# A Fourier mixer on 256 token rows instead of 512, and a modulation that comes one place later

## What is computed

```python
e = rms_norm(p @ w_ple_proj, ple_norm_gain)
x = x + sigmoid(x @ w_ple_gate) * e
...
mod = silu(c) @ w_ada[i] + b_ada[i]
sh1, sc1, g1, sh2, sc2, g2 = split(mod, 6)
h = rmsnorm(x, norm_mix_g) * (1 + sc1) + sh1
hg = h.reshape(B, S, 4, 256)
f = fft.fftn(hg, axes=(1, 3), norm="ortho").real
x = x + g1 * (f.reshape(B, S, 1024) @ w_fourier_out)
h = rmsnorm(x, norm_ffn_g) * (1 + sc2) + sh2
x = x + g2 * swiglu(h, w_ffn_in, w_ffn_out)
```

## Time and profile before

| what | us |
|---|---|
| median of 3 runs | 1541.34 (1540.82 to 1541.92) |
| the profiled execution | 1540.15 |
| its span in the trace | 1538.2 |
| PE busy in the span | 1526.9 |
| DVE, ACT, POOL busy | 786.8, 632.4, 876.3 |
| from the first gate residual on DVE to the last square sum | 299.4 to 320.3 |
| first matmul of the Fourier output | 342.28 |

### The profile page before, as it was taken

One profiled execution on the slowest core, in us unless ns is written; L12 is line 12 of the kernel. 1 busy time (PEld: TensorE's weight loads), 2 busy tenths in 40 slices (PEclk: granted clock), 3 DMA queues, 4 the chain that ended last, 5 costly groups with the idle time before them and its releaser, 6 DMA issues.

```text
span 1538.2 us, 21352 instructions
## 1 busy us (share of the span) xinstructions
PE 1526.9 (99%) x7242; PEld 1276.9 (83%) x7242; DVE 786.8 (51%) x1176; ACT 632.4 (41%) x1038; POOL 876.3 (57%) x1040
## 2 busy tenths in 40 slices
PE   9999999999999999999999999999999999999997
PEld 7888888898888888888888888888889888888886
DVE  7887787876654544541554435356257454011113
ACT  7444444674533333323444334253345333122223
POOL 6555557556577766775454535526435766555551
PEclk9999999999999999999999999999999999999999
DMA  7544455335355555542232322213312553222321
GB/s 247 178 145 165 167 192 191 110 110 178 122 180 205 196 190 181 199 150 96 101 103 69 108 69 94 95 52 96 95 55 83 205 205 123 96 96 95 95 82 55
DMA packets 58267, 202.99 MB, mean 132 GB/s; under 512 B 6496, under 2 KB 8544, under 8 KB 58208
## 3 DMA queue, kind: packets, MB, share of 16 engines
q1 hardware_dynamic: 56912, 198.87, 37.8%
q10 hardware_dynamic: 1296, 3.30, 0.6%
HBM read 200.05 MB, written 2.10 MB: 131 GB/s over the span
## 4 chain that ended last, share of the span: by engine, by line
PE 78%; POOL 11%; issue 9%; ACT 0%; DMA 0%; DVE 0%; SPq 0%; POOLq 0%; DVEq 0%; ACTq 0%
PE banks L1785 21%; PE banks L1789 21%; PE banks L1788 21%; POOL w_lo L423 11%; PE banks L2270 2%; PE banks L2269 2%; PE banks L2266 2%; PE banks L1801 2%; PE banks L1804 2%; PE banks L1805 2%; PE banks L2306 1%; PE banks L2304 1%; PE banks L2305 1%; PE banks L2293 0%; PE banks L2292 0%
## 5 line engine op out<-in xcount | busy, mean ns | idle before, releaser
L423 POOL TENSOR_TENSOR w_lo<-w_raw,w_hi 128x256 fp32r<-128x256 f32 x1028 | 868.9, 877 | 627.8 <-ACT w_hi L455 627.7
L455 ACT ACTIVATE w_hi<-w_raw 128x1024 fp32r<-128x1024 f32 x257 | 269.9, 1057 | 582.6 <-PE banks L1785 518.8
L1785 PE MATMUL banks<-a_hi,w_lo 128*128 128x512 f32 x1224 | 479.2, 391 | 0.1
L1789 PE MATMUL banks<-a_hi,w_hi 128*128 128x512 f32 x1224 | 476.7, 389 | 0.0
L1788 PE MATMUL banks<-a_lo,w_hi 128*128 128x512 f32 x1224 | 476.6, 389 | 0.0
L1785 PEld LDWEIGHTS banks<-a_hi,w_lo 128*128 128x128 f32 x1224 | 230.1, 188 | 47.6 <-issue 0.8
L1789 PEld LDWEIGHTS banks<-a_hi,w_hi 128*128 128x128 f32 x1224 | 229.8, 188 | 47.8
L1788 PEld LDWEIGHTS banks<-a_lo,w_hi 128*128 128x128 f32 x1224 | 229.9, 188 | 47.3 <-issue 0.2
L1785 PE MATMUL banks<-b_hi,w_lo 128*128 128x512 f32 x562 | 219.6, 391 | 0.0
L1789 PE MATMUL banks<-b_hi,w_hi 128*128 128x512 f32 x562 | 218.8, 389 | 0.0
L1788 PE MATMUL banks<-b_lo,w_hi 128*128 128x512 f32 x562 | 218.8, 389 | 0.0
(11 more groups left out here) (300 smaller groups left out, 1708.4 us busy)
## 6 DMA issues: line engine op xcount, KB each, us to landing
w_raw<-in_W SPq DMA_DIRECT2D x258, 512.0 KB, 3.5
ada_raw<-in_ADA SPq DMA_DIRECT2D x112, 512.0 KB, 4.2
X<-in_XT SPq DMA_DIRECT2D x8, 256.0 KB, 6.3
scr<-in_DECAY ACTq DMA_DIRECT2D x4, 448.0 KB, 3.9
out<-X SPq DMA_DIRECT2D x7, 256.0 KB, 2.2
w_raw<-in_W SPq DMA_DIRECT2D x2, 256.0 KB, 3.9
scr<-in_PT ACTq DMA_DIRECT2D x1, 512.0 KB, 4.8
scr<-in_ROPE ACTq DMA_DIRECT2D x1, 512.0 KB, 4.5
```

The source lines that it names most:

```text
L423: pool.tensor_tensor(w_lo[:, c % RING, part], w_raw[:, c % RING, part], w_hi[:, c % RING, part].bitcast(fp32), ALU.subtract).then_inc(wlo, 1)
L455: act.activation(w_hi[:, c % RING, :], w_raw[:, c % RING, :], ACT.Copy).then_inc(whi, 1)
L1785: mm = pe.matmul(out, lo, x_hi, start=first, stop=False)
L1789: mm = pe.matmul(out, hi, x_hi, start=False, stop=last)
```

## The change

**Folding.** The transform over tokens t and 512-t uses that their cosines are equal and their sines opposite. XH and XL are written with tokens 0 to 256 straight and 511 to 257 reversed behind them, in two operations each, so that a token's partner stands in the same row of another block. After `dft1` of a group, ACT scales the reversed half (`mirrored`), DVE adds it to and subtracts it from the other half in place (`token_pairs`: 129 columns of sums, 127 of differences), and ACT and DVE split the result (`sums_hi`, `sums_lo`). Token 256 has no partner: its row goes through two one-row matmuls with a row of alternating signs (`middle_token`, `alternating`). `dft2` then has 2 chunks, 24 sine, 24 cosine and 6 edge matmuls, and 10 one-row matmuls for the middle token (2 for each group's cosines, 2 for the edges); the order is sine 0, cosine 0, sine 1, 2, 3, edges, cosine 1, 2, 3.

**Norm.** The last square sum goes to `rinv` in two halves in the same token order, and `rinv_columns` runs behind group 1.

**Splits.** The splits of gate chunks 4 and 5 move from the gate's loop to behind the mixed input's tiles 5 and 6. The gate's hook runs at product 32 instead of 30.

**Modulation.** Vector 4 goes through `ada_fold`, `ada_move` and `ada_collect` in the output product; the eight steps of vector 5 leave the Fourier stage, and each later vector is made one place later, with four steps among the residuals of the second down product.

The diff, cut to its core:

```diff
-for _name, _n in (("body", 8 * NH), ("out", 8), ("ple", 2), ("gate", 8), ("dft1", 1), ("dft2", 4), ("fout", 8),
+for _name, _n in (("body", 8 * NH), ("out", 8), ("ple", 2), ("gate", 8), ("dft1", 1), ("dft2", 2), ("fout", 8),
...
+                r = c + min(max(c - CH["dft2"], 0), 2)
...
-            straight(*[0] * 8, 1, 1, 0, 0, 0, 1, 1, 1, 1, 1, 1)
-            assert pos[1] == 6 * KD
+            until(CH["dft2"])
+            straight(0, 0)
             until(CH["up0a"] + 10)
-            turns(6 * KD // 4, 4, 1)
+            turns(7 * KD // 4, 4, 1)
...
-                if m == 4:
-                    split_w(flat, CH["ple"] + 5)
+                if 4 <= m < 7:
+                    split_w(flat, CH["ple"] + m + 1)
...
-                ins = act.activation(XH[:, m, :], X[:, m, :], ACT.Identity, bias=zero,
-                                     scale=gs[:, KD + m:KD + m + 1])
+                for dst, src in ((XH[:, m, 0:MID], X[:, m, 0:MID]), (XH[:, m, MID:S], X[:, m, S - 1:MID - 1:-1])):
+                    ins = act.activation(dst, src, ACT.Identity, bias=zero, scale=gs[:, KD + m:KD + m + 1])
...
-                if n not in (3, 7):
+                if n not in (0, 1, 3, 7):
...
+                    act.activation(alternating[:, 0:NF - 2:2], ones[0:1, 0:P], ACT.Copy)
+                    act.activation(alternating[:, 1:NF - 2:2], ones[0:1, 0:P], ACT.Copy, scale=-1.0)
+                    act.activation(alternating[:, NF - 2:NF], ones[0:1, 0:2], ACT.Copy).then_inc(signs, 1)
...
-            for z in range(2 * NH):
-                wait_tile(act, flat, t1 + z)
-                for h in range(2):
-                    half, tt = slice(2 * P * h, 2 * P * (h + 1)), 2 * (z % 2) + h
-                    ins = act.activation(a_hi[:, z, half], banks[:, BANK[t1 + z], half], ACT.Identity, bias=zero,
-                                         scale=rcol[:, tt:tt + 1])
-                ins.then_inc(z_hi, 1)
-                if z == 3:
-                    wait_tile(act, flat, t1 + 2 * NH - 1)
-                    split_w(flat, c0 + 4, free=True)
+
+            def mirrored(g):
+                wait_tile(act, flat, t1 + 2 * g + 1)
+                src, dst = banks[:, BANK[t1 + 2 * g + 1], :], FM[:, g % 2, :]
+                act.activation(dst[:, 2 * P:S], src[:, 2 * P:S], ACT.Identity, bias=zero, scale=rcol[:, 3:4])
+                if g == 0:
+                    act.wait_ge(mid_ready, 1)
+                act.activation(dst[:, 0:2 * P], src[:, 0:2 * P], ACT.Identity, bias=zero, scale=r_mid)
+                act.activation(half_hi_row[0:1, 2 * P * g:2 * P * g + P + 1], src[0:1, 0:P + 1], ACT.Identity,
+                               bias=zero[0:1], scale=rcol[0:1, 2:3]).then_inc(z_mirrored, 1)
+
+            def sums_hi(g):
+                act.wait_ge(z_sum, g + 1)
+                act.activation(a_hi[:, 2 * g, :], banks[:, BANK[t1 + 2 * g], :], ACT.Copy).then_inc(z_hi, 1)
+
+            mirrored(0)
+            for g in range(1, NH):
+                mirrored(g)
+                sums_hi(g - 1)
+            split_w(flat, c0 + 4, free=True)
+            sums_hi(NH - 1)
...
-                if m == 2:
-                    ada_out(AUX["ada4"], 4)
...
-                dve.scalar_tensor_tensor(out=XL[:, m, :], in0=X[:, m, :], scalar=gs[:, KD + m:KD + m + 1],
-                                         in1=XH[:, m, :].bitcast(fp32), op0=ALU.mult,
-                                         op1=ALU.subtract).then_inc(xl, 1)
+                for n, src in enumerate((X[:, m, 0:MID], X[:, m, S - 1:MID - 1:-1])):
+                    part = slice(MID, S) if n else slice(0, MID)
+                    ins = dve.scalar_tensor_tensor(out=XL[:, m, part], in0=src, scalar=gs[:, KD + m:KD + m + 1],
+                                                   in1=XH[:, m, part].bitcast(fp32), op0=ALU.mult, op1=ALU.subtract)
+                ins.then_inc(xl, 1)
...
+                if m < KD - 1:
+                    read_out(dve.tensor_tensor(sqsum[:, :], sqsum[:, :], bank, ALU.add), t0 + m)
+                else:
+                    dve.tensor_tensor(rinv[:, 0:MID], sqsum[:, 0:MID], bank[:, 0:MID], ALU.add)
+                    read_out(dve.tensor_tensor(rinv[:, MID:S], sqsum[:, S - 1:MID - 1:-1], bank[:, S - 1:MID - 1:-1],
+                                               ALU.add), t0 + m)
...
+            def token_pairs(g):
+                dve.wait_ge(z_mirrored, g + 1)
+                low, high = banks[:, BANK[td + 2 * g], :], banks[:, BANK[td + 2 * g + 1], :]
                 for h in range(2):
-                    half, tt = slice(2 * P * h, 2 * P * (h + 1)), 2 * (z % 2) + h
-                    ins = dve.scalar_tensor_tensor(out=a_lo[:, z, half], in0=banks[:, BANK[td + z], half],
-                                                   scalar=rcol[:, tt:tt + 1], in1=a_hi[:, z, half].bitcast(fp32),
-                                                   op0=ALU.mult, op1=ALU.subtract)
-                read_out(ins, td + z)
+                    for first, last, op in ((0, P + 1, ALU.add), (P + 1, 2 * P, ALU.subtract)):
+                        part = slice(2 * P * h + first, 2 * P * h + last)
+                        ins = dve.scalar_tensor_tensor(out=low[:, part], in0=low[:, part], scalar=rcol[:, h:h + 1],
+                                                       in1=FM[:, g % 2, part], op0=ALU.mult, op1=op)
+                ins.then_inc(z_sum, 1)
+                row = slice(2 * P * g, 2 * P * g + P + 1)
+                read_out(dve.scalar_tensor_tensor(out=half_lo_row[0:1, row], in0=high[0:1, 0:P + 1],
+                                                  scalar=rcol[0:1, 2:3], in1=half_hi_row[0:1, row].bitcast(fp32),
+                                                  op0=ALU.mult, op1=ALU.subtract), td + 2 * g + 1)
+
+            def sums_lo(g):
+                dve.wait_ge(z_hi, g + 1)
+                read_out(dve.tensor_tensor(a_lo[:, 2 * g, :], banks[:, BANK[td + 2 * g], :],
+                                           a_hi[:, 2 * g, :].bitcast(fp32), ALU.subtract), td + 2 * g)
+
+            token_pairs(0)
+            for g in range(1, NH):
+                token_pairs(g)
+                sums_lo(g - 1)
+            sums_lo(NH - 1)
...
-            ada(k=3)
+            ada_fold(4)
...
+                        ada_collect(4)
...
+                        ada(k=4)
+                        ada_fold(7)
...
-                        residuals(t, range(KD - 1), g0 + 5, v)
+                        ada(k=2)
+                        for m in range(KD - 1):
+                            residuals(t, (m,), g0 + 5, v)
+                            if m < 2:
+                                ada()
...
-                    if m == 3:
-                        ada_columns(flat, AUX["ada4"], 4)
...
-                if n == 30:
+                if n == 32:
...
-                    mm = pe.matmul(aux[:, tt:tt + 1], sqsum[:, tt * P:(tt + 1) * P], ones[:, 0:1], start=True, stop=True)
+                    mm = pe.matmul(aux[:, tt:tt + 1], rinv[:, tt * P:(tt + 1) * P], ones[:, 0:1], start=True, stop=True)
...
-                if g == 2:
+                if g == 1:
...
+            def middle_token(out, rows):
+
+                pe.matmul(out, half_lo_row[0:1, rows], alternating, start=False, stop=False)
+                return pe.matmul(out, half_hi_row[0:1, rows], alternating, start=False, stop=True)
...
+                t = t1 + 2 * g + 1
+                out = banks[:, BANK[t], 0:NF]
+                wait_bank(flat, t)
+                for h in range(2):
+                    o = 2 * P * h
+                    token_sums(out, a_hi[:, 2 * g, o:o + P], a_lo[:, 2 * g, o:o + P], h, 1, False, False)
+                if g == 0:
+                    pe.wait_ge(signs, 1)
+                wait_read(pe, flat, td + 2 * g + 1)
+                middle_token(out, slice(2 * P * g, 2 * P * g + P)).then_inc(tile_ready, 2)
...
+            cosine_sums(0)
             sine_sums(1)
-            cosine_sums(0)
```

More of the change, by code:

```diff
@@ L105 @@
 _c = 0
-for _name, _n in (("pre", 1), ("body", 7 * NH), ("post", 1), ("ada4", 1), ("ple", 1), ("four", 1), ("fshift", 1), ("edge", 1),
+for _name, _n in (("pre", 1), ("body", 7 * NH), ("post", 1), ("ple", 1), ("four", 1), ("fshift", 1), ("edge", 1),
                   ("ffn0", 1), ("rnorm", 1),
@@ L215, in build @@
         XH, XL = b_hi, b_lo
+        MID = S // 2 + 1
+        half_hi_row, half_lo_row = (b[:, 8:10, :].rearrange("p k s -> p (k s)") for b in (b_hi, b_lo))
+        alternating = b_hi[0:1, 11, 0:NF]
+        r_mid = small[:, 21:22]
         RPRE, RPRE2 = area(16), area(17)
@@ L439, in _ @@
                     lo_part(at, 4 + s)
-            for c in range(4 * n, N_CHUNK):
+            for c in range(4 * n, N_LOAD):
                 lo_part(flat, c)
@@ L474, in vector, with ada_move @@
                 return lambda m: mod[:, KD * g + m:KD * g + m + 1]
+            def ada_move(g, at=flat):
+                act.wait_ge(ada_folded, at("vector", g - 3))
```

(36 more changed lines are left out.)

150 lines of the change are left out of this document (68 added, 82 removed).

## The result

The changed kernel takes 1543.20 us (median; the kernel before 1541.22 over as many runs): the ratio is 1.0015, interval 1.0009 to 1.0021. It is slower by 2.0 us where 3.0 less was forecast. The profiled execution took 1543.13, span 1541.3; that of before lay 1.1 under its median, so the spans differ by 3.1. The following readings are of these two executions.

A forecast was written before the change was run, and what follows sets the result against it. PE, busy 99%, bounds the whole, but DVE's and ACT's chain decides before the Fourier output. PE saves 7.2 us, waits take 4.2: -3.0, median 1538.3 us, range 1535.4 to 1542.9.

The forecast's parts named there:

- PE's saving: Deleted and replaced matmuls on PE: could end 7.2 us earlier if nothing were late; waits take 4.2 of it.
- the modulation: Vector 4's new path and later vectors made one place later: costs nothing, hidden by residuals' waits on PE.
- (a): Gate's tail: moved splits' GpSimd pieces collide with DVE, residual of summed squares +1.8 us, inverse root +0.9.
- (b): Low parts of the folded input, written by DVE in two halves a tile: last square sum +1.0 us.
- the rival with both halves blocked at each tile: Folded input's low parts: GpSimd blocks both DVE halves, 1.87 us a tile, total +4.6, 1545.9; chance 0.08.
- (c): From the inverse root to the edge rows: norm's columns at 321.65, edge rows end at 336.3.
- (d): From edge rows to Fourier output: 3.3 us of untouched ACT and DVE work, output starts at 339.6, -2.7.
- the two waits: PE waits 1.4 us at the gate's statistics and some 2 us before the norm's columns.
- the chain's 3.3: ACT and DVE work from the last edge matmul to the Fourier output, 3.3 us; PE's cosines end within it.
- The second wait of the output: In the Fourier output product, PE's wait for the input's second part goes: -0.3 us.
- The rival "no collision": Gate's tail: the moved pieces don't collide with DVE, (a) becomes -0.2, total -4.1, 1537.2; chance 0.17.

The follow-up runs named there:

- kernel 5: kernel 2 with the gate's statistics hook at product 30 instead of 32; 1539.12 us, ratio 0.9993 to the kernel before.
- kernel 10: kernel 5 with the splits of gate chunks 4 and 5 where the change puts them; 1542.49 us, ratio 1.0009.
- kernel 9: the change with matmuls of no use filling both of PE's long waits, at statistics and norm's columns; 1542.59 us.
- kernel 4: the change without the one-row matmuls for the middle token; 1542.43 us, one run.
- kernel 7: the kernel before with only the modulation part of the change, no folding; 1541.29 us, ratio 1.0001.
- kernel 1: the change with the splits of gate chunks 4 and 5 back in the gate's loop; 1543.94 us, ratio 1.0018.
- kernel 8: the change with 16 matmuls of no use ahead of the norm's columns; 1543.10 us, ratio 1.0011.
- kernel 6: the change with the folded input's low parts written whole and straight, one operation a tile; 1542.51 us, one run.
- kernel 2: kernel 1 with the sign operations earlier and the table load ahead of the inverse root left out; 1542.76 us, ratio 1.0012.
- kernel 11: kernel 5 with group 2's sums split before group 3 is touched, the weight split behind the last sums; 1539.48 us, ratio 0.9992.

## Why the prediction was wrong

The frame was right. The stretch became bound by DVE's and ACT's chain, PE's saving turned into waits at the places named, the modulation was nearly free. The sum went wrong by 5.1 us at the output's start (344.70 against 339.6), in sizes that all missed to the same side:

- **(a), the step that failed: +0.9 for the root, measured +2.7.** The eight pieces met nearly everything: the residual came 3.1 late, where 1.8 was taken and 4.3 was the bound. The mixing operations lost 1.8 (1.6 was taken), some of it out of a wait that DVE had before, but the additions lost 1.6 instead of 0.2. They were to have slack because they "wait for ACT's squares". The rows of before show the reverse: DVE waited 0.35 once, ahead of the first addition, and from then on ACT waited for DVE (0.24 at 284.39). The prediction also forgot that the sign operations stand ahead of the root's table load, which ended at 294.81, some 0.4 behind the statistics. That is some 0.4 of the 2.7. The price of the moved splits is shown by kernels 5 and 10: 3.4 us, more than the whole forecast gain.
- **(b): +1.0, measured +2.2.** Without a collision a tile's two halves take 0.80 from their start to that of the next instruction, as predicted (0.79). But three of seven tiles met GpSimd (1.36 for the two halves) where one had before, 0.9 more; and ACT's two halves, put at nothing, take 1.08 instead of 0.80 and made DVE wait 0.35 at the first tile (305.23). Of the rival with both halves blocked at each tile (1.87) nothing was seen, but it had the right mechanism.
- **(c) and (d): 18.0 from the columns to the output, measured 20.1.** 1.1 is the half clock (kernel 9), which the prediction did not have at all, though it named the two waits. The other 1.0 is PE's own work, read in kernel 5 at full clock. Its edge rows end 15.0 behind the columns instead of 14.65, since the sine matmuls of groups 2 and 3 stand ahead of them. The last three cosine sums take 4.05 from there instead of 3.0, since a pair of one-row matmuls costs 0.62 instead of 0.24. So PE ended last, and not the chain's 3.3 (kernel 4).
- **The second wait of the output**, which was to save 0.3, grew by 0.3 (1.87 us from the first matmul to the seventh, 1.60 before), **and the modulation cost 0.4** (kernel 7). Both were taken at their best.

These make up the difference: 1.7 + 1.2 + 2.1 = 5.0 at the output's start, and 0.6 + 0.4 = 1.0 behind it. Of the profiled executions 3.0 less was forecast and their spans differ by 3.1 the other way, 6.1 in all. The rival "no collision" is what kernel 5 comes near to: its root ended at 292.7 and its output, at 340.3, lies 0.7 from the forecast; its time, 1539.1, is still 1.9 above that rival's 1537.2. The cause of the slower kernel is thus late statistics, and in the change it is the moved splits that make them late. Kernel 1 shows that the splits cannot just be put back: with the hook at product 32 the wait for chunk 4 holds the statistics as long.

On the one-row matmuls the Trainium skill ("TensorE: Matmul & The Clock Gate", section "Why this matters for your kernels") says that a single matmul over 32 rows takes the time of one over 128. No run here has 32 rows. With one row the duration agrees, but for the first behind a switch (0.28 for the one-row matmul at 341.80 as for the full one at 341.37). The starts do not agree where few and full rows alternate: around a pair of one-row matmuls, and around one of 33 rows, some 0.4 us are lost in all.

## What to carry to other kernels

Work that is moved out of a critical engine's way must be followed to whom it triggers: here two ACT operations of 1 us each, put into an idle place, sent GpSimd into DVE's last operations ahead of a statistic that everything waits for. An estimate of "some will collide" between two bounds lay near the bad end here, where the other engine's work came back to back, and the slack that it leaned on is read from who waits for whom. And a saving on the engine that is busy 99% is worth nothing until the next wait on it is known: kernel 7 deletes 1.7 us from PE and gets none of them.

## What was not expected of the hardware

- *Half clock after a short wait.* Waits of 2.55 and 1.72 us in the change were followed by 3.3 us at a granted clock of 0.50 each, from about 1 us after PE's return; with PE kept busy in both there was none (kernel 9), nor behind waits of 1.0 and 0.8 (kernel 5). The length of the wait does not settle it: behind 2.54 in kernel 8, 2.51 in kernel 4 and 2.31 in kernel 2 the clock stayed at 1.00, and behind 1.38 in kernel 6 it was 0.50 for some six us.
- *A tiny operation that waits for several pieces.* In kernel 11's profiled execution an operation on 128x8 elements took 2.38 us beside GpSimd's sixteen pieces in a row (1.69 in kernel 7's), in kernel 5's 0.28, and the last square sum came 2 us later than in kernel 5:

```profile
298.49 2.38 DVE L1439 SCALAR_TENSOR_TENSOR shift_hl<-mod,shift_hl 128x8 fp32r<-128x8 f32 x1
```

```profile
298.58 0.28 DVE L1437 SCALAR_TENSOR_TENSOR shift_hl<-mod,shift_hl 128x8 fp32r<-128x8 f32 x1
```

  The Trainium skill ("SBUF — State Buffer", section "SBUF: two separate sides") has the loser of the shared port pair wait for the whole instruction that holds it. The row fits that and seems to say more: 2.1 us above 0.28 is about three pieces of 0.7, as if DVE had lost several in a row. Neither this nor whether it is why the times of kernels 5 and 11 spread over 4 us was tried.
